# Output products of the first mixer in another order around the conformer's statistics

## The reference, cut to what matters

```python
y_conf = conformer_conv(conf_ab, w_conf_dw[i], conf_ln_g[i], conf_ln_b[i], w_conf_pw[i])
y_att = forgetting_attention(q, k, v, f_logit + b_forget[i])
y_sc = short_conv_mixer(sc_h, sc_b, sc_c, w_sc[i])
y_pool = multiscale_pool(pool_v, w_pool[i], pool_scale[i])
mix = jnp.concatenate([y_conf, y_att, y_sc, y_pool], axis=-1) @ w_out[i]
h = h + rms_norm(mix, g_mix_post[i])
hn = rms_norm(h, g_mlp_pre[i])
```

## Time and profile before

| | |
|---|---|
| median of 3 runs | 946.85 us (946.34 to 947.07) |
| the profiled execution | 946.72 us |
| its span from the first to the last instruction | 944.9 us |
| TensorE busy | 932.7 us, 99% of the span |
| VectorE, ScalarE, GpSimd busy | 683.2, 513.0, 93.4 us |
| TensorE's mean granted clock | 0.999 of full speed |

### The profile page before, as it was taken

The page is one execution under the profiler, slowest core; times in us unless marked ns, Lnnn a source line. Parts: engine busy times, 40 slices in busy tenths (PEclk is TensorE's granted clock), DMA queues, the critical chain, the costliest instruction groups (busy, mean ns, idle before and its releaser), DMA issues.

```text
span 944.9 us, 12903 instructions
## 1 busy us (share of the span) xinstructions
PE 932.7 (99%) x5197; PEld 810.9 (86%) x5197; DVE 683.2 (72%) x921; ACT 513.0 (54%) x692; POOL 93.4 (10%) x113
## 2 busy tenths in 40 slices
PE   9999999999999999999999999999999999999997
PEld 8997888888888898788888888889998888888885
DVE  5899857666657977966766766558999767666664
ACT  5887545444446656954544334368685545334432
POOL 3550200000011101100000000000243010000000
PEclk9999999999999999999999999999999999999999
DMA  9933666566646355146666565556423457656531
GB/s 290 342 127 126 195 229 216 187 202 193 203 151 201 112 189 179 45 134 223 223 195 205 177 184 179 175 159 219 137 90 113 134 157 248 218 179 194 179 117 45
DMA packets 106955, 167.00 MB, mean 177 GB/s; under 512 B 2896, under 2 KB 82848, under 8 KB 106768
## 3 DMA queue, kind: packets, MB, share of 16 engines
q1 hardware_dynamic: 104400, 157.71, 51.3%
q0 software_dynamic: 2208, 7.95, 2.4%
q10 hardware_dynamic: 288, 0.52, 0.1%
HBM read 165.13 MB, written 1.05 MB: 176 GB/s over the span
## 4 chain that ended last, share of the span: by engine, by line
PE 84%; DVE 9%; DMA 2%; issue 2%; ACT 2%; POOL 0%; POOLq 0%; DVEq 0%; ACTq 0%
PE ps L399 82%; PE ps L407 3%; DVE wl L1921 2%; DMA raw<-in_w_in 2%; DVE SC L2052 1%; ACT wh L1316 1%; DVE fs L2062 1%; DVE SC L2037 0%; DVE wl L1935 0%; ACT junk L1304 0%; DVE xhl L1982 0%; DVE wl L2092 0%; DVE hs L1964 0%; DVE xf L2626 0%; DVE h L2005 0%
## 5 line engine op out<-in xcount | busy, mean ns | idle before, releaser
L1921 DVE TENSOR_TENSOR wl<-raw,wh 128x2048 fp32r<-128x2048 f32 (+2 forms) x141 | 318.1, 2260 | 142.8 <-ACT wh L1316 142.7
L1316 ACT ACTIVATE wh<-raw 128x2048 fp32r<-128x2048 f32 (+2 forms) x150 | 281.9, 1886 | 155.9 <-PE ps L399 137.9
L399 PE MATMUL ps<-xhl,wh 128*128 128x512 f32 (+1 forms) x1248 | 254.8, 351 | 0.0
L399 PEld LDWEIGHTS ps<-xhl,wh 128*128 128x128 f32 x1248 | 199.4, 190 | 26.1
L399 PE MATMUL ps<-wh,xhl 128*128 128x512 f32 (+3 forms) x800 | 190.9, 380 | 0.2 <-DVE xhl L1944 0.2
L399 PEld LDWEIGHTS ps<-wh,xhl 128*128 128x128 f32 x800 | 142.7, 188 | 25.2 <-DVE xhl L1944 0.7
L399 PEld LDWEIGHTS ps<-xhl,wl 128*128 128x128 f32 x1008 | 135.7, 191 | 7.5
L399 PE MATMUL ps<-xhl,wl 128*128 128x256 f32 x1008 | 140.6, 283 | 0.0
L399 PE MATMUL ps<-wl,xhl 128*128 128x512 f32 (+3 forms) x403 | 102.2, 375 | 0.2 <-DVE wl L1935 0.2
L399 PE MATMUL ps<-wh,fh 128*128 128x512 f32 x304 | 91.1, 393 | 0.3 <-DVE fl L2292 0.3
L399 PE MATMUL ps<-wh,fl 128*128 128x512 f32 x304 | 90.2, 390 | 0.0
(11 more groups left out here) (300 smaller groups left out, 820.4 us busy)
## 6 DMA issues: line engine op xcount, KB each, us to landing
raw<-in_ffn_gate SPq DMA_DIRECT2D x22, 1024.0 KB, 5.4
raw<-in_ffn_up SPq DMA_DIRECT2D x22, 1024.0 KB, 5.4
raw<-in_ffn_down SPq DMA_DIRECT2D x22, 1024.0 KB, 4.9
raw<-in_w_up SPq DMA_DIRECT2D x16, 1024.0 KB, 5.5
raw<-in_w_down SPq DMA_DIRECT2D x16, 1024.0 KB, 5.0
raw<-in_s_w_in SPq DMA_DIRECT2D x14, 1024.0 KB, 5.3
raw<-in_w_in SPq DMA_DIRECT2D x9, 1024.0 KB, 9.8
raw<-in_a_w_in SPq DMA_DIRECT2D x6, 1024.0 KB, 5.6
```

The lines of the kernel that those rows point to most:

```text
L399: return e.matmul(o, a, b, start=start, stop=stop, skip_group_check=True)
L1316: e.activation(high_of(i), raw_of(i), ACT.Copy).then_inc(*up("act_high", i))
L1921: e.tensor_tensor(low_of(i), raw_of(i), high_of(i).bitcast(F32), ALU.subtract).then_inc(*up("dve_lo", i))
```

## The change

It touches the first mixer alone. On TensorE, products of the output weight are split by passes (`part`) and take other places. On VectorE, the sum of the conformer's two tap accumulators goes ahead of the first tap of the short convolution. The conformer's output is no longer copied to SBUF: ScalarE writes its high part, block by block, from PSUM, and VectorE makes the low part from PSUM.

```diff
                 project(1, sl, 3, 0, order, at("dve_mix_low", 3, 0))
+                def part(i, tb, x, w, first=False):
+                    for c in range(2):
+                        for k in range(2):
+                            d = mm(ps[ACC[1][tb][c]][:, :], x[:, 2 * i + k, tokens(tb)], weight(sl[i])[w][:, k, HALF[c]],
+                                   first and k == 0, False)
+                    return d
+                e.wait_ge(*at("dve_mix_low", 3, 1))
+                part(3, 1, xh, 0, True)
+                part(3, 1, xl, 0)
                 conformer_mean()
-                e.wait_ge(*at("dve_mix_low", 3, 1))
-                project(1, sl, 3, 1, order)
+                part(3, 1, xh, 1).then_inc(*up("pe_slot", sl[3]))
                 e.wait_ge(*at("dve_short_out"))
                 forget_mix(1)
+                e.wait_ge(*at("act_part_high", 1, 2, 0))
+                e.wait_ge(*at("act_high", sl[2]))
+                part(2, 0, xh, 0)
                 conformer_variance()
                 e.wait_ge(*at("dve_forget_max", 3, 1))
                 forget_turn(2)
+                e.wait_ge(*at("act_part_high", 1, 2, 1))
+                part(2, 1, xh, 0)
+                e.wait_ge(*at("dve_mix_low", 2, 0))
+                part(2, 0, xl, 0)
                 forget_turn(3)
-                e.wait_ge(*at("act_part_high", 1, 2, 0))
-                project(1, sl, 2, 0, order, at("dve_mix_low", 2, 0))
+                e.wait_ge(*at("dve_mix_low", 2, 1))
+                part(2, 1, xl, 0)
+                e.wait_ge(*halves_ready(sl[2]))
+                part(2, 0, xh, 1)
                 forget_mix(2)
                 e.wait_ge(*at("act_conf_std"))
                 forget_mix(3)
-                for c in range(2):
-                    for k in range(2):
-                        mm(ps[ACC[1][1][c]][:, :], xh[:, 4 + k, tokens(1)], weight(sl[2])[0][:, k, HALF[c]], False, False)
                 conformer_out()
+                part(2, 1, xh, 1).then_inc(*up("pe_slot", sl[2]))
                 ...
                     project_half(1, sl, 0, 0, half, at("dve_mix_low", 0, 0))
-                e.wait_ge(*at("dve_mix_low", 2, 1))
-                for c in range(2):
-                    for k in range(2):
-                        mm(ps[ACC[1][1][c]][:, :], xl[:, 4 + k, tokens(1)], weight(sl[2])[0][:, k, HALF[c]], False, False)
-                for c in range(2):
-                    for k in range(2):
-                        d = mm(ps[ACC[1][1][c]][:, :], xh[:, 4 + k, tokens(1)], weight(sl[2])[1][:, k, HALF[c]], False, False)
-                d.then_inc(*up("pe_slot", sl[2]))
...
                 e.wait_ge(*at("pe_conf_out"))
-                e.activation(xf[:, 0:2, :], ps[3][:, :].rearrange("p (t n) -> p t n", t=2), ACT.Copy).then_inc(
-                    *up("act_conf_out"))
-                e.wait_ge(*at("act_conf_out"))
                 for tb in range(2):
-                    part_high(0, 2, tb, (1, 0, tb))
+                    e.activation(xh[:, 0:2, tokens(tb)], ps[3][:, :].rearrange("p (t n) -> p t n", t=2)[:, :, tokens(tb)],
+                                 ACT.Copy).then_inc(*up("act_part_high", 1, 0, tb))
...
                 taps(25, TAPS)
+                taps_sum()
                 for k in (1, 2):
                     for t in range(2):
-                        if (k, t) == (1, 1):
-                            taps_sum()
...
-                mix_low(0)
+                e.wait_ge(*at("act_part_high", 1, 0, 1))
+                for tb in range(2):
+                    s = tokens(tb)
+                    e.tensor_tensor(xl[:, 0:2, s], ps[3][:, :].rearrange("p (t n) -> p t n", t=2)[:, :, s],
+                                    xh[:, 0:2, s].bitcast(F32), ALU.subtract).then_inc(*up("dve_mix_low", 0, tb))
```

## The result

The changed kernel takes 948.91 us in the median of 21 runs (946.81 to 950.6), the kernel before, timed beside it, 946.85 (946.25 to 948.4). The ratio on record is 1.0015, with a 95% interval of 1.0010 to 1.0021: slower by 1.4 us, 0.9 to 2.0, so 948.3 against the 947.4 that was forecast. The two medians themselves lie 2.1 apart and the two means 1.7 (948.72 and 947.03), so the size of the loss is known only as something between 1 and 2 us. The interval excludes a gain, and its end lies at the 0.2% that the prediction took as its bound. The profiled execution took 948.07, its span is 946.3, TensorE's mean granted clock 0.998.

A forecast was written before the change was run, and what follows sets the result against it. TensorE, busy 99%, bounds the kernel, but around the change the first norm's fixed chain after block 0's sums decides. Those sums come 0.69 us later: 946.72 + 0.69 gives 947.4 us, range 946.4 to 948.6, without the gain and clock rivals.

The forecast's parts named there:

- The hole at the mean: TensorE's 1.50 us wait before the conformer's mean, for VectorE's sum of taps; claimed to go, filled by eight products.
- the rival in which those products themselves wait (948.5): At the mean: the moved products wait, the mean stays put, block 0's sums come 1.8 us later; chance 0.03.
- The tap sum's price, 0.1: On VectorE: the earlier tap sum loses some overlap, delaying everything behind it by 0.1 us, between 0 and 0.2.
- the output at 89.42: Conformer's output on TensorE: waits for ScalarE's SiLU, so starts at 89.42 at best, only 0.23 before its old 89.65.
- the 0.69: First mixer: block 0's sums complete at 97.55 instead of 96.86, 0.69 us later, and all behind moves by the same.
- Block 0's sums later by the spent cover: First mixer: eight of the 26 products covering the norm's chain are spent earlier, so the sums come 0.69 us later.
- The split hidden: Conformer's output split from PSUM: gain or loss, at the latest 0.2 us later, hidden behind 3.6 us of products.
- the norm's chain of fixed length: First norm, from block 0's sums to its transposes: 6.12 us on the other engines, unchanged.
- a wait of 2.0 at the transposes: First norm's transposes: TensorE arrives at 101.64 and waits 2.0 us until 103.67, formerly half a microsecond.
- The gain comes through: Rival at the norm: its chain is shorter than its rows, the 1.50 hole is won, 945.4 us; chance 0.07.
- the SiLU slips by half a microsecond: Rival at ScalarE's SiLU: waits ahead of the second map's copy delay output and block 0's sums, 947.9 us; chance 0.14.
- The clock falls in the new wait: Rival at the norm's transposes: TensorE's clock halves after the 2.0 us wait, adding 2.55 us, 950.0; chance 0.04.

The follow-up runs named there:

- e2: Changed kernel with all eight of slot 2's last block 1 products back behind block 0's sums: 946.91 us, ratio 1.0000 to the kernel before.
- e1: Changed kernel with slot 2's four low-weight products of block 1 back behind block 0's sums: 946.88 us, ratio 0.9996 to the kernel before.
- e8: Kernel before with only the conformer's output split from PSUM, a single run: 946.97 us (before 947.0).
- e7: The changed kernel run again, unaltered, for another profile and more granted clocks: 948.77 us, ratio 1.0014 to the kernel before.
- e4: Changed kernel with slot 1's twelve block 1 products also ahead of block 0's last ones, lengthening the wait: 951.49 us, ratio 1.0049 to the kernel before.
- e9: e2 with a shorter chain to the conformer's SiLU, output products in their old order: 945.45 us, ratio 0.9984 to the kernel before.
- e5: Changed kernel with eight unread filler products in the wait ahead of the norm's transposes: 947.79 us, ratio 1.0013 to the kernel before.
- e6: e2 with the shorter SiLU chain and the output's four products reordered, which gives a wrong result: 945.7 us, ratio 0.9986 to the kernel before.
- e10: Kernel before with the shorter SiLU chain alone, none of the moved products: 946.25 us, ratio 0.9993 to the kernel before.

## Why the prediction came out as it did

- **The hole at the mean is filled, without a new wait.** Right: the mean starts behind its eight new products, and the rival in which those products themselves wait (948.5) fell with it.
- **The tap sum's price, 0.1, and the output at 89.42.** On before's clock VectorE's normalised rows come 0.13 later than in before (87.58 for 87.45) and the SiLU begins at 88.31, so the price was about right:

```profile
87.49 0.69 DVE L2206 TENSOR_TENSOR SC<-SC 128x512 f32<-128x512 f32 x1
...
88.22 1.09 ACT L1510 ACTIVATE SC<-SC,prm 128x256 f32<-128x256 f32 x2
```

  The output starts at 89.54, 0.14 behind the end of the SiLU's 1.09, where 0.05 had been put for the release. That the SiLU bounds it was right: e2's 0.86 is that bound, seen directly. These 0.12 are the larger part of the 0.18 to 0.19 that the 0.69 fell short by; the output's own 1.61 us (91.06 − 89.45), where 1.54 had been put, is the rest.
- **Block 0's sums later by the spent cover.** Right in kind: 0.87 at the second square instead of 0.69. The sum charged the four products that came in behind the output (28 instead of 24, with their slow start 0.92) and took off the 0.23 by which the output was to come sooner; measured are 0.98 and 0.11. The sentence beside the sum names all eight products that left the cover as the reason, and that is looser than the sum: e1 and e2 show that the four ahead of the output cost nothing, and the four behind it 0.9, which is 4 × 0.227.
- **The split hidden, the norm's chain of fixed length, a wait of 2.0 at the transposes, an even shift from there.** Right: e8; 5.92 to 5.94 in all eleven traces; 1.89; +0.90 and +0.91 at 130 and 300 us. It is not even to the end: behind 318 us 0.5 is added by something else (last section).
- **The gain comes through; the SiLU slips by half a microsecond.** Refuted: in after nothing is won at the transposes, and the output starts 0.11 earlier than in before.
- **The clock falls in the new wait: this is the step that failed.** It was given 0.04 and 2.55 us. It happens in about half of the executions (10 of 21, 7 of 11) and costs 1.0; the prediction's own sign of being wrong, a granted clock under 1.00 behind the wait, is in the traces of e7 and e4. Together, 0.9 and half of 1.0 is 1.4, the ratio's figure, and 0.3 to 0.7 under what the means and the medians give. That 948.3 lies inside the forecast's range is in part luck: the range left the clock out, and reached high enough only for the sake of the SiLU and the moved products, neither of which came; the median, 948.9, lies above it. The prediction had read "between 1.50 and 3 us, and the trace speaks for the far end" from one fall, at the end of the span. Such a fall is one sample. In e1, whose last product begins at 938.03, in the same stretch as that of before, the granted clock is down earlier, in 940 to 941 us, where before had 1.00 until 942:

```profile
938.03 0.39 PE L399 MATMUL ps<-wl,fh 128*128 128x512 f32 x1
```

```profile
939.00:940.00 1.00, 0.00 (x0) 0.00 (x0) 0.90 (x3) 0.72 (x2) 0.00 (x0) 1.00 0.00 0
940.00:941.00 1.00, 0.00 (x0) 0.00 (x0) 0.34 (x2) 0.20 (x1) 0.55 (x1) 0.72 0.00 0
```

  The same idle engine keeps its clock for a shorter or a longer time, and so it is with the wait of 1.9 here: in after the clock stayed at 1.00, in e7 it fell. The price was too high because the whole stretch behind the wait was doubled; in e7 and e4 the low clock held for 3.41 us, whether TensorE had waited 1.9 or 4.6, and 1.0 us of that reached the end. The rule of the Trainium skill that the prediction weighed ("TensorE: Matmul & The Clock Gate", section "HAM oscillation — how this bites in real kernels": halved when idle too long, paid again on return) is borne out by e7 and e4, with 0.50 behind the wait. It was the prediction's reading of the trace, "not in so short a wait", that was wrong.

What of the runs stays open: the 11 runs of after at 0.998 or more have a median 1.2 above before, where the trace gives 0.9 (e7's four such runs 0.6). Falls that the count missed, and the first item of the last section, may be in it; neither was measured run by run.

## What to carry to other kernels

Work that covers a fixed chain on other engines is a stock: filling a hole with it pays only if the end of the hole, and not the chain, is the next limit, so ask of each moved product on which side of the next binding wait it will stand. When two waits bind within a microsecond, undo them together or not at all; here either alone gave nothing, and e9, which has both, gained 0.8 us. And gathering idle time in one place can cost more than its length, since TensorE's clock may fall there: price that from several executions' granted clocks, not from one fall in one trace.

## What the runs showed of the hardware

**One GpSimd operation has two durations.** In the gate's norm, behind 318 us, the same power of 128 values took 1.53 us in five profiled executions (after, e2, e4, e5, e8) and 0.93 in seven, and in the first five everything behind it came 0.5 us later; the kernel does not decide it, as after and e7 are the same. After, then e7:

```profile
319.21 1.53 POOL L2781 TENSOR_TENSOR st<-st,prm 128x1 f32<-128x1 f32 x1 [6.78 <-DVE st L2002]
```

```profile
320.24 0.93 POOL L2781 TENSOR_TENSOR st<-st,prm 128x1 f32<-128x1 f32 x1 [6.77 <-DVE st L2002]
```

It explains the profiled execution of after: 0.9 + 0.5 is the 1.4 by which it stands above that of before. So that this 1.4 equals the ratio's is a coincidence. What decides between the two durations was not tried.

**A wait of VectorE that nothing releases.** In before and after VectorE stands for 0.46 us at 380 and at 600 us with nothing but its own last operation ahead. In e6, e9 and e10, which have one VectorE instruction more (the halves of the scaling), it does not, and the shift gains 0.3 to 0.4 us at each place: e10's −0.66 at 900 us, and e9's further −0.65 there, come from this, not from the mixer. Before, then e10:

```profile
598.45 1.28 DVE L2247 TENSOR_REDUCE SC<-ps 128x256 f32<-128x512 f32 x2
600.19 0.69 DVE L2283 TENSOR_TENSOR SC<-SC 128x512 f32<-128x512 f32 x1 [0.46 <-DVE SC L2247]
```

```profile
597.90 1.28 DVE L2248 TENSOR_REDUCE SC<-ps 128x256 f32<-128x512 f32 x2
599.29 0.69 DVE L2284 TENSOR_TENSOR SC<-SC 128x512 f32<-128x512 f32 x1
```

That the place depends on the count of instructions ahead would fit, but no run was made to try it.
